# Two mixers of a four-layer fp32 network: weight chunks in another order, transposes that take turns by a table, and a key selection cut in three

## The chip, the cores and the metric

The kernel runs on one core of a Trainium2 chip. The metric is the device time of one launch in microseconds (us). The program computes, for one sequence of 256 tokens of width 1024, two layers of a first block and two layers of a second, and reads 458 MB of weights while it does so.

## The reference, cut to what matters

Every layer is a gated feed-forward, a mixer and a second feed-forward. The first block's mixer projects the normalized input to fifteen groups of columns and runs three attentions on them; the second block's mixer runs a state-space branch and one latent attention.

```
def hybrid_mixer(h, ...):                       # first block
    proj = h @ w_in
    (qa, ka, va, qi, ki, wi, qb, kb, vb, qc, kc, vc, ga, gb, gc) = jnp.split(proj, ...)
    qa, ka = rope(rmsnorm(qa)), rope(rmsnorm(ka)); qi, ki = rope(qi), rope(ki)
    o_a = dsa_attention(qa, ka, va, qi, ki, wi)  # index scores, the 64 best keys of each query, then attention
    o_b = moba_attention(rope(rmsnorm(qb)), rope(rmsnorm(kb)), vb)
    o_c = diff_attention(rope(rmsnorm(qc)), rope(rmsnorm(kc)), vc, lam, ...)
    merged = sigmoid(ga) * (o_a @ wa) + sigmoid(gb) * (o_b @ wb) + sigmoid(gc) * (o_c @ wc)
    return merged @ w_out

for l in range(2):                               # second block
    h = h + 0.5 * swiglu(rms_norm(h), ...)
    z, xbc, dt_raw, cq, ckv, kr, gates = split_cols(rms_norm(h) @ w_in, ...)
    y_ssd = ssd_branch(z, xbc, dt_raw, ...)      # causal convolution, chunked scan, norm, projection
    y_mla = mla_branch(cq, ckv, kr, ...)         # cq -> 8 heads of q, ckv -> k and v, rope, attention
    h = h + (g[:D] * y_ssd + g[D:] * y_mla) @ w_o
    h = h + 0.5 * swiglu(rms_norm(h), ...)
```

All of it is fp32. The kernel splits every weight and every activation into a high and a low part, and a product is three matmuls.

## The kernel before

The program is twelve phases: feed-forward, m1, feed-forward, feed-forward, m1, feed-forward for the first block and the same with m2 for the second. m1 is the first block's mixer (phases 1 and 4), m2 the second's (phases 7 and 10). Weights arrive as chunks of at most 1 MB (128 partitions, 2048 columns) in the order that chunk_list (L46) gives. The sync engine (SP) sends each chunk to one of five RAW slots; the scalar engine (ACT) rounds each half of it to WHI (`hi`, L1438, four slots); the vector engine (DVE) subtracts and writes the low part over RAW as WLO (`lo`, L2345); then TensorE (PE) multiplies. A chunk's slot is given back when PE has spent it.

Each engine runs a list of calls that is written out by hand (Tensor.m1 at L652, Scalar.m1, Vector.m1, Pool.m1, and the same for m2). An engine does its list strictly in order and meets the others by semaphores alone: `up` counts, `at` is the value to wait for. So a call that waits holds up all that is behind it on its engine.

m1 has 13 chunks called at (projections), then 12 called ag (gates), then ab and ao (output). A projection chunk j goes through these hands:

- PE: `at_`, four pieces of 12 matmuls (L390 to L392) into a PSUM bank;
- ACT: `tev`, copy to a staging slot of STA (three slots), and `psq`, squares to JUNK;
- DVE: `pss` (L2560, L2562), the sums of squares; for some chunks `kn` (L2571), which runs three Newton steps (L2350 to L2358) and scales the staging slot;
- GpSimd (POOL): `pg` (L3460, gain, and L3445 to L3449, rope, through RTA), and for the query chunks `prs` (L3477 to L3495), Newton steps on 128x8 numbers in 15 small instructions;
- PE: `ptr` (L518), four transposes of the staged slot, after which `sc` (scores, L557), `pt` and `pv` work on the attention's units 0 to 11: A (units 0, 1 and their like), B, then C from unit 6 on.

Between the index scores (`ix`, L535) and attention A stands the selection: `top`, eight rounds of MAX8 and MATCH_REPLACE8 on DVE (L2617, L2619) for each of two query blocks, 247.09 to 261.67 us.

m2 has four chunks bt (latent projections), 12 bx (convolution, `cv` L2922 on DVE), three bq and two bk (queries, keys and values from the latent), eight bz, and then bg, bs, bm, bo. Its q and k halves are staged in STB (four slots), transposed by `qtr`, `ktr` and `kptr` (helper L946), and the POOL engine does `qg` (L3573 and L3550 to L3554, gain and rope of a 128x512 tile), `rq` (L3582, L3584, the Newton steps, L3587) and `kp` (L3595). One PSUM bank serves all the transposes in turn, in the order of the table M2_TR.

Matmul groups are named by these lines: L379 to L381 are the gate, convolution and z chunks and the feed-forwards, L390 to L392 the projections.

Of the kernel before, what the change touches and what calls it, by code (L numbers as in the profile page):

```python
# [14 lines left out]
P = 128  # L15
# [29 lines left out]

def chunk_list(phases):  # L46

    out = []
    for kind, f in phases:
# [7 lines left out]
        elif kind == "m1":  # L57
            out += [("at", f, j) for j in range(13)]
            out += [("ag", f, j) for j in range(12)]
            out += [("ab", f, j) for j in range(3)] + [("ao", f, 0), ("ab", f, 3)]  # L60
            out += [("ao", f, j) for j in range(1, 4)]
        else:
            out += [("bt", f, j) for j in range(4)]
            out += [("bx", f, j) for j in range(8, 12)]
            out += [("bq", f, j) for j in range(3)]
            out += [("bk", f, j) for j in range(2)]
            for g in range(4):
                out += [("bx", f, 2 * g), ("bx", f, 2 * g + 1), ("bz", f, 2 * g), ("bz", f, 2 * g + 1)]
# [67 lines left out]
class Counts:  # L136
# [6 lines left out]
    def before(self, member, distance):  # L143
# [4 lines left out]
M1_ALL = (0, 1, 2, 3, 4, 5, 7, 8, 9, 10)  # L148
M1_BANK = Counts([0, 1] + list(range(3, 13)))
M1_STAGE = Counts(M1_ALL)  # L150
M1_SQUARE = Counts([2, 3, 4, 5, 7, 8, 9, 10, "sn0", "sn1"])
# [14 lines left out]
M1_TR = Counts(list(M1_ALL) + ["sn0", "sn1"])  # L166

M2_UNITS = [(0, (0, 2, 4, 6)), (0, (1, 3, 5, 7)), (1, (0, 2)), (1, (1, 3)), (1, (4, 6)), (1, (5, 7))]
M2_BANK = Counts([("bt", j) for j in range(4)] + [("bx", j) for j in range(8, 12)] + [("bq", j, t) for j in range(3) for t in range(2)]
                 + [("bk", j, t, h) for j in range(2) for t in range(2) for h in range(2)]  # L170
                 + [(kind, j) for g in range(4) for kind in ("bx", "bz") for j in (2 * g, 2 * g + 1)])
M2_TR = Counts([("lat", 0), ("lat", 1), ("lat", 2), ("cb", 0), ("cb", 1), ("q", 0, 0), ("cb", 2), ("q", 0, 1), ("cb", 3),
                ("q", 1, 0), ("q", 1, 1), ("dt",), ("btt",), ("q", 2, 0), ("q", 2, 1), ("k", 0, 0), ("k", 0, 1), ("kp", 0),
                ("k", 1, 0), ("k", 1, 1), ("kp", 1)]
               + [(kind, g) + c for g in range(4) for kind, c in (("xdt", (0,)), ("xdt", (1,)), ("s", ()), ("y", ()))])
# [4 lines left out]
M2_CONV = Counts(list(range(8, 12)) + list(range(8)))  # L180


def build(nc, phases, x_in, pos_in, w_in, cf_in, cm1_in, cm2_in, out, ctx):
# [61 lines left out]
    RTA = sb("RTA", [P, 2, 256], F32, at_kb(91.5))  # L245
# [109 lines left out]
    def m1_bank(j):  # L355
        return PS[6 if j == 2 else 4 + M1_BANK.index[j] % 2]

# [10 lines left out]
    class Tensor:  # L368
# [129 lines left out]
        def at_(self, n, j, t, p):  # L498
            e = self.e
            if t == p == 0 and j in M1_BANK.index and M1_BANK.index[j] > 1:  # L500
                e.wait_ge(*at("tev", n, M1_BANK.before(j, 2)))
            w = M1W[j]
            ins = self.columns(m1_bank(j)[:, t * 256:t * 256 + w], n, ck(n, "at", j), w, t, p, j == 0)
            ins.then_inc(*up("at", n, j, t, p))

        def ptr(self, n, j):
# [7 lines left out]
            if M1_TR.before(j, 1) is not None:  # L514
                e.wait_ge(*at("qt", n, M1_TR.before(j, 1)))
# [5 lines left out]
        def ix(self, n, t, u):  # L521
# [3 lines left out]
            if r == 0:  # L525
                e.wait_ge(*at("qt", n, 1))
                e.wait_ge(*at("qt", n, 2))
# [10 lines left out]
        def sc(self, n, i, x):  # L538
# [38 lines left out]
        def pv(self, n, i):  # L577
# [3302 lines left out]
```

## Time and profile before

| | us |
|---|---|
| median of three runs | 2791.62 (2791.45 to 2792.38) |
| the profiled execution | 2792.47 |
| its span | 2790.7 |
| mean granted clock of TensorE | 0.991 |
| PE busy | 2732.8 (98%) |
| DVE busy | 1788.0 (64%) |
| ACT busy | 1435.3 (51%) |
| POOL busy | 291.6 (10%) |

The span is the time from the first to the last instruction; some 1.8 us of the execution's own time lie outside of it. PE is the engine that works all the time, and the question of this kernel is where it does not: span less busy is 58 us. In the tables of stretches a row gives the length of the stretch and then, for each engine, busy time and number of instructions; the number behind the five engines is the granted clock of PE, 1.00 being 2.4 GHz and 0.5 being 1.2 GHz. POOL is nearly idle, and yet its small steps stand in chains on which PE waits.

### The profile page before, as it was taken

To read this page: it belongs to the slowest core of one execution; us is meant where nothing else is said; L and a number is where in the kernel's file an instruction comes from. 1 tells how busy PE (TensorE), PEld (TensorE's weight loads), DVE (VectorE), ACT (ScalarE), POOL (GpSimd) and SP (SyncE) were. 2 spreads that over 40 slices of the span, in tenths; PEclk is the share of its full clock that TensorE was granted. 3 is DMA by queue.
4 is the path that set the end of the run, shared out by engine and by line. 5 is a ranking of instruction groups with operands and counts; after the bars stand their busy time and mean duration, and the time that the engine had idled before them with its cause. 6 is when DMAs were issued, how large, how long until landed. Compare 5 with 4: busy or idle time off the path is not lost.

```text
span 2790.7 us, 48889 instructions
## 1 busy us (share of the span) xinstructions
PE 2732.8 (98%) x20056; PEld 2573.8 (92%) x20056; DVE 1788.0 (64%) x3060; ACT 1435.3 (51%) x2445; POOL 291.6 (10%) x446
## 2 busy tenths in 40 slices
PE   8999999999999999999999899999999999999999
PEld 8998999999998999999998899999999988999998
DVE  5558857456568856556558687565565596875654
ACT  5445645444445645445446575454454565854543
POOL 0005211000005210000002212100000022111000
PEclk9999999999999999999999999999999999999999
DMA  5453254554543344545444234554444442345453
GB/s 206 184 200 127 107 181 161 192 196 174 190 176 122 122 177 176 193 168 196 182 158 167 89 137 152 181 184 181 181 182 181 177 162 91 128 160 181 167 185 147
DMA packets 64733, 462.02 MB, mean 166 GB/s; under 512 B 7296, under 2 KB 7808, under 8 KB 9344
## 3 DMA queue, kind: packets, MB, share of 16 engines
q1 hardware_dynamic: 64512, 458.90, 44.9%
q8 instruction: 160, 2.62, 0.4%
q14 instruction: 61, 0.50, 0.1%
HBM read 457.83 MB, written 1.05 MB: 164 GB/s over the span
## 4 chain that ended last, share of the span: by engine, by line
PE 85%; POOL 5%; DVE 4%; issue 3%; ACT 1%; DMA 1%; SPq 0%; DVEq 0%; POOLq 0%; ACTq 0%
PE bank L457 17%; PE bank L379 17%; PE bank L381 17%; PE bank L380 17%; PE bank L390 3%; PE bank L392 3%; PE bank L391 3%; PE bank L645 3%; DVE WLO L2345 1%; DVE CV L2922 1%; PE bank L423 1%; DMA RAW<-weights_dram 1%; POOL STA L3460 1%; POOL SM L3485 1%; POOL SM L3483 0%
## 5 line engine op out<-in xcount | busy, mean ns | idle before, releaser
L2345 DVE TENSOR_TENSOR WLO<-RAW,WHI 128x1024 fp32r<-128x1024 f32 (+1 forms) x872 | 1056.9, 1251 | 282.4 <-ACT WHI L1438 281.0
L1438 ACT CAST WHI<-RAW 128x1024 fp32r<-128x1024 f32 (+1 forms) x872 | 885.5, 1047 | 374.9 <-DMA RAW<-weights_dram 238.4
L379 PE MATMUL bank<-XH,WHI 128*128 128x256 f32 x3712 | 1064.1, 287 | 4.0 <-DVE WLO L2345 4.0
L380 PE MATMUL bank<-XL,WHI 128*128 128x256 f32 x3712 | 1052.2, 283 | 0.0
L381 PE MATMUL bank<-XH,WLO 128*128 128x256 f32 x3712 | 1052.0, 283 | 0.0
L379 PEld LDWEIGHTS bank<-XH,WHI 128*128 128x128 f32 x3712 | 713.7, 192 | 13.1 <-issue 5.8
L380 PEld LDWEIGHTS bank<-XL,WHI 128*128 128x128 f32 x3712 | 713.9, 192 | 6.6 <-issue 1.4
L381 PEld LDWEIGHTS bank<-XH,WLO 128*128 128x128 f32 x3712 | 713.5, 192 | 0.0
L1502 ACT ACTIVATE SG<-bank 128x256 f32<-128x256 f32 x152 | 58.4, 384 | 481.9 <-PE bank L381 481.9
L2458 DVE TENSOR_TENSOR HF<-SG,bank 128x256 f32<-128x256 f32 x152 | 64.0, 421 | 339.1 <-ACT SG L1502 339.1
L390 PE MATMUL bank<-WHI,XH 128*128 128x256 f32 (+2 forms) x928 | 268.8, 290 | 5.0 <-DVE XL L2399 4.9
L392 PE MATMUL bank<-WHI,XL 128*128 128x256 f32 (+2 forms) x928 | 263.6, 284 | 0.0
L391 PE MATMUL bank<-WLO,XH 128*128 128x256 f32 (+2 forms) x928 | 263.5, 284 | 0.0
L457 PE MATMUL bank<-WHI,HH 128*128 128x512 f32 x704 | 219.4, 393 | 0.0
L457 PE MATMUL bank<-WLO,HH 128*128 128x512 f32 x704 | 217.8, 390 | 0.0
L457 PE MATMUL bank<-WHI,HL 128*128 128x512 f32 x704 | 217.4, 390 | 0.0
L390 PEld LDWEIGHTS bank<-WHI,XH 128*128 128x128 f32 x928 | 179.2, 193 | 7.3 <-issue 6.5
L391 PEld LDWEIGHTS bank<-WLO,XH 128*128 128x128 f32 x928 | 179.5, 193 | 0.4
L392 PEld LDWEIGHTS bank<-WHI,XL 128*128 128x128 f32 x928 | 179.4, 193 | 0.0
L457 PEld LDWEIGHTS bank<-WLO,HH 128*128 128x128 f32 x704 | 132.2, 188 | 29.0
L457 PEld LDWEIGHTS bank<-WHI,HL 128*128 128x128 f32 x704 | 132.2, 188 | 28.5
L457 PEld LDWEIGHTS bank<-WHI,HH 128*128 128x128 f32 x704 | 123.0, 189 | 17.0
(346 smaller groups left out, 3190.7 us busy)
## 6 DMA issues: line engine op xcount, KB each, us to landing
RAW<-weights_dram SPq DMA_DIRECT2D x431, 1024.0 KB, 4.8
RAW<-weights_dram SPq DMA_DIRECT2D x2, 800.0 KB, 4.2
X<-x_dram SPq DMA_DIRECT2D x2, 512.0 KB, 6.0
RAW<-weights_dram SPq DMA_DIRECT2D x2, 512.0 KB, 7.5
out_dram<-X SPq DMA_DIRECT2D x2, 512.0 KB, 2.7
RAW<-weights_dram SPq DMA_DIRECT2D x2, 384.0 KB, 3.2
CM<-mixer_dram SPq DMA_DIRECT2D x2, 320.5 KB, 9.8
CM<-mixer_dram SPq DMA_DIRECT2D x2, 176.0 KB, 5.3
```

What stands on the lines that cost most here:

```text
L379: self.e.matmul(bank, h, xh[:, x0 + k, :], start=k == k0, stop=False)
L380: self.e.matmul(bank, h, xl[:, x0 + k, :], start=False, stop=False)
L381: ins = self.e.matmul(bank, l, xh[:, x0 + k, :], start=False, stop=k == k1)
L390: self.e.matmul(bank, xh[:, x0 + k, xs], h, start=k == k0, stop=False)
L391: self.e.matmul(bank, xh[:, x0 + k, xs], l, start=False, stop=False)
L392: ins = self.e.matmul(bank, xl[:, x0 + k, xs], h, start=False, stop=k == k1)
L457: ins = e.matmul(PS[2 * t + nh][:, :], a[:, i % HR, t * P:t * P + P], w[:, c % s, col + nh * 512:col + nh * 512 + 512], start=i == 0 and w ...
L645: ins = e.matmul(PS[2 * t + h][:, :], a[:, k, xs], w[:, c % s, i * 1024 + h * 512:i * 1024 + h * 512 + 512], start=k == 0 and w is WHI and ...
L1438: e.copy(WHI[:, c % NHI, a:b], RAW[:, c % NLO, a:b]).then_inc(*up("hi", c, p))
L1502: e.activation(SG[:, i % 2, :], PS[5 - i % 2][:, 0:256], ACT.Silu).then_inc(*up("sg", n, i))
L2345: e.tensor_tensor(WLO[:, c % NLO, a:b], RAW[:, c % NLO, a:b], WHI[:, c % NHI, a:b].bitcast(F32), ALU.subtract).then_inc(*up("lo", c, p))
L2458: e.tensor_tensor(HF[:, r, :], SG[:, r, :], PS[5 - i % 2][:, 256:512], ALU.mult).then_inc(*up("hf", n, i))
```

## The change

The order of chunks in both mixers becomes a table, and banks, staging slots and waits are derived from the tables. In m1 the gate chunk ag0 now comes behind at11, ag1 to ag3 behind at5, ag4 and ag5 behind at12, and ag6 to ag11 at the end; the projections stand in the order 1, 0, 2, 3, 6, 9, 11, 4, 10, 5, 12, 7, 8. In m2, bx and bz chunks come between the latent chunks; bk1, which makes the second half of the keys' and values' input, is late. Attention C of m1 moves behind ag7. Transposes follow their own tables. RTA has three buffers in place of two. `top` takes the first and last round, and is called three times for each query block. The lists of the five engines follow from that. Cut to its core:

```
+M1_ORDER = [("at", 1), ("at", 0), ("at", 2), ("at", 3), ("at", 6), ("at", 9), ("at", 11), ("ag", 0), ("at", 4), ("at", 10), ("at", 5), ...]
+M1_TRANSPOSED = [0, 1, 2, 3, 9, 4, 10, 5, 7, 8]
+M2_ORDER = [("bt", 0), ..., ("bt", 3), ("bx", 9), ("bq", 0), ("bq", 1), ("bq", 2), ("bk", 0), ("bx", 8), ("bz", 0), ("bx", 0), ("bx", 1), ("bk", 1), ...]
+M2_TRANSPOSED = [("lat", 0), ("lat", 1), ("lat", 2), ("q", 0, 0), ("q", 0, 1), ("q", 1, 0), ("q", 1, 1), ("q", 2, 0), ("k", 0, 0), ("k", 0, 1), ("q", 2, 1), ("kp", 0), ...]
...
-            out += [("at", f, j) for j in range(13)]
-            out += [("ag", f, j) for j in range(12)]
+            out += [(k, f, j) for k, j in M1_ORDER]
...
-    RTA = sb("RTA", [P, 2, 256], F32, at_kb(91.5))
+    RTA = sb("RTA", [P, 3, 256], F32, at_kb(91.5))
...
+        def m1_tr_free(self, n, m):
+            if M1_TR.before(m, 1) is not None:
+                self.e.wait_ge(*m1_tr_read(n, M1_TR.before(m, 1)))
...
-        def top(self, n, t, rounds, end):
+        def top(self, n, t, a, z):
...
-            for _ in range(rounds):
+            for _ in range(a, z):
...
# Vector.m1
-            self.top(n, 0, 8, True)
+            self.top(n, 0, 0, 3)
+            self.top(n, 0, 3, 6)
+            self.top(n, 0, 6, 8)
             self.causal(n, 1)
-            self.top(n, 1, 8, True)
-            self.pss(n, 4)
-            self.pss(n, 5)
-            self.nb(n, 0)
-            self.pss(n, 7)
-            self.kn(n, 5)
+            self.top(n, 1, 0, 3)
+            self.top(n, 1, 3, 6)
+            self.top(n, 1, 6, 8)
+            self.pss(n, 9)
...
# Pool.m1
             self.prs(n, 3)
+            self.pg(n, 9)
+            self.prs(n, 9)
             self.pg(n, 4)
+            self.pg(n, 10)
+            self.prs(n, 4)
             self.pg(n, 5)
             self.pg(n, 7)
-            self.prs(n, 4)
             self.prs(n, 7)
             self.pg(n, 8)
-            self.pg(n, 9)
-            self.prs(n, 9)
-            self.pg(n, 10)
# Pool.m2
             self.qg(n, 1)
+            self.kp(n, 0)
             self.rq(n, 0)
+            self.kp(n, 1)
             self.rq(n, 1)
-            self.kp(n, 0)
-            self.kp(n, 1)
...
# Tensor.m1, behind the index scores
             self.ptr(n, 3)
+            self.at_(n, 9, 1, 0)
+            self.at_(n, 9, 1, 1)
+            self.at_(n, 11, 0, 0)
...
+            self.sc(n, 0, 0)
+            self.sc(n, 0, 1)
+            self.ag(n, 0, 0, 0)
...
+            self.ptr(n, 9)
+            self.at_(n, 4, 0, 0)
...
+            self.at_(n, 10, 1, 1)
+            self.ptr(n, 4)
```

Three places of the lists, first as before and then as changed. On DVE behind the selection of the first m1 (SBI is its result; JUNK holds the squares):

```order
L2622 TENSOR_SCALAR SBI<-ISC 128x256
L2560 TENSOR_REDUCE SM<-JUNK 128x8
L2562 TENSOR_SCALAR SM<-SM 128x8
L2560 TENSOR_REDUCE SM<-JUNK 128x8
L2562 TENSOR_SCALAR SM<-SM 128x8
L2636 TENSOR_REDUCE SM<-bank 128x2 x2
L2648 SCALAR_TENSOR_TENSOR SM<-SM 128x4
```

```order
L2657 MATCH_REPLACE ISC<-SM,ISC 128x256
L2660 TENSOR_SCALAR SBI<-ISC 128x256
L2598 TENSOR_REDUCE SM<-JUNK 128x8
L2600 TENSOR_SCALAR SM<-SM 128x8
L2383 TENSOR_TENSOR WLO<-RAW,WHI 128x1024 x6
L2598 TENSOR_REDUCE SM<-JUNK 128x8
L2600 TENSOR_SCALAR SM<-SM 128x8
L2383 TENSOR_TENSOR WLO<-RAW,WHI 128x1024 x2
L2674 TENSOR_REDUCE SM<-bank 128x2 x2
```

Six `lo` now stand directly behind one sum of squares (that of at9), and two more behind the next; before, the first `lo` came only behind three sums and the Newton steps of kn5. On POOL, from the last instruction of prs3 on (STA is the staging tile, RTA the rope's scratch, SM small numbers):

```order
L3495 TENSOR_SCALAR SM<-SM 128x8
L3460 TENSOR_TENSOR STA<-STA,CM 128x512
L3445 TENSOR_TENSOR RTA<-STA,CC_61 128x128
L3446 TENSOR_TENSOR RTA<-STA,SS_62 128x8x8
L3447 TENSOR_TENSOR RTA<-STA,SS_62 128x8x8
L3449 TENSOR_TENSOR STA<-RTA 128x8x16
L3460 TENSOR_TENSOR STA<-STA,CM 128x512
```

```order
L3549 TENSOR_SCALAR SM<-SM 128x8
L3514 TENSOR_TENSOR STA<-STA,CM 128x512
L3503 TENSOR_TENSOR RTA<-STA,CC_61 128x128
L3504 TENSOR_TENSOR RTA<-STA,SS_62 128x8x8
L3505 TENSOR_TENSOR RTA<-STA,SS_62 128x8x8
L3507 TENSOR_TENSOR STA<-RTA 128x8x16
L3531 TENSOR_SCALAR SM<-SM 128x8
L3532 TENSOR_SCALAR SM<-SM 128x8
L3535 TENSOR_TENSOR SM<-SM 128x8
```

Where pg5 followed pg4 directly, the 15 instructions of prs9 now stand between pg9 and pg4. On POOL in m2, around the first scaling of the keys' rope part, kp (STB is the staging tile):

```order
L3485 TENSOR_SCALAR SM<-SM 128x8
L3487 TENSOR_TENSOR SM<-SM 128x8
L3587 TENSOR_SCALAR SM<-SM 128x8
L3595 TENSOR_TENSOR STB<-SM_67,SM 128x512 x2
L3603 TENSOR_TENSOR JUNK<-XDT,SM_67 128x512
```

```order
L3608 TENSOR_TENSOR STB<-RT_122 128x512
L3653 TENSOR_TENSOR STB<-SM_67,SM 128x512
L3639 TENSOR_TENSOR SM<-SM 128x8
L3641 TENSOR_SCALAR SM<-SM 128x8
L3531 TENSOR_SCALAR SM<-SM 128x8
L3532 TENSOR_SCALAR SM<-SM 128x8
```

The first kp moved ahead of both rq and stands directly behind the second rope; the second kp stands between rq0 and rq1.

## Rows read from the trace of the kernel before

**Rows 1.** The page's busy times: engine, us, share of the span, instructions.
```profile
PE 2732.8 (98%) x20056; PEld 2573.8 (92%) x20056; DVE 1788.0 (64%) x3060; ACT 1435.3 (51%) x2445; POOL 291.6 (10%) x446
```
**Rows 2.** Stretches: both m1, a feed-forward, both m2; PE, PEld, DVE, ACT, POOL, clock, DMA.
```profile
203.00:450.00 247.00, 236.84 (x1813) 223.75 (x1811) 180.75 (x407) 136.93 (x259) 69.87 (x125) 0.99 0.41 145
450.00:637.00 187.00, 187.00 (x1334) 176.65 (x1333) 104.03 (x148) 87.16 (x130) 0.00 (x0) 1.00 0.50 183
826.00:1072.00 246.00, 236.71 (x1807) 223.63 (x1807) 180.62 (x404) 136.38 (x256) 69.85 (x125) 0.98 0.40 144
1448.00:1836.00 388.00, 375.12 (x2876) 352.71 (x2875) 290.13 (x507) 229.98 (x439) 73.46 (x95) 0.98 0.41 146
2212.00:2598.00 386.00, 371.97 (x2877) 350.05 (x2876) 290.39 (x508) 230.02 (x438) 73.41 (x95) 0.99 0.41 146
```
**Rows 3.** Waits of 203 to 450 us: who for whom, total, number, longest.
```profile
PE bank L518 <- DVE STA L2571: 5.6, 2, 5.2
```
**Rows 4.** DVE in time order, first m1: start, duration.
```profile
247.09 0.28 DVE L2617 MAX8 SM<-ISC 128x8 f32<-128x128 f32 x1
261.67 0.68 DVE L2560 TENSOR_REDUCE SM<-JUNK 128x8 f32<-128x512 f32 x1
269.88 2.36 DVE L2345 TENSOR_TENSOR WLO<-RAW,WHI 128x1024 fp32r<-128x1024 f32 x2
```
**Rows 5.** POOL in time order, first m1.
```profile
244.11 0.95 POOL L3433 MEMSET QT<- 128x1024 f32 x1 [4.64 <-PE bank L535]
245.15 0.44 POOL L3477 TENSOR_SCALAR SM<-SM 128x8 int32<-128x8 int32 x1
250.45 1.30 POOL L3460 TENSOR_TENSOR STA<-STA,CM 128x512 f32<-128x512 f32 x1
253.36 1.35 POOL L3460 TENSOR_TENSOR STA<-STA,CM 128x512 f32<-128x512 f32 x1
270.09 1.06 POOL L3483 TENSOR_TENSOR SM<-SM 128x8 f32<-128x8 f32 x1
```
**Rows 6.** PE in time order: two matmuls 48 apart in m1; transposes in m2.
```profile
256.66 0.28 PE L390 MATMUL bank<-WHI,XH 128*128 128x256 f32 x1
262.42 0.28 PE L390 MATMUL bank<-WHI,XH 128*128 128x256 f32 x1
1480.88 0.60 PE L913 MATMUL bank<-CF,CQ 128*128 128x128 f32 x4
1518.52 0.60 PE L946 MATMUL bank<-CF,STB 128*128 128x128 f32 x4
1521.73 0.60 PE L972 MATMUL bank<-BC 128*128 128x128 f32 x4
```
**Rows 7.** Stretches at a low granted clock, columns as in Rows 2.
```profile
268.00:276.00 8.00, 6.78 (x33) 5.09 (x34) 5.05 (x13) 2.12 (x4) 6.38 (x20) 0.57 0.01 2
1538.00:1542.00 4.00, 3.08 (x10) 1.73 (x8) 3.76 (x11) 3.37 (x5) 3.23 (x10) 0.57 0.01 2
1551.00:1559.00 8.00, 5.11 (x26) 5.11 (x27) 1.94 (x2) 1.70 (x3) 3.75 (x3) 0.57 0.01 2
2312.00:2320.00 8.00, 4.04 (x21) 4.04 (x21) 2.69 (x3) 1.16 (x2) 4.66 (x5) 0.57 0.00 0
```
**Rows 8.** PE's longest wait in m2: 1448 to 1836 us, then 2212 to 2598 us.
```profile
PE bank L946 <- POOL STB L3595: 4.9, 1, 4.9
...
PE bank L946 <- POOL STB L3595: 5.5, 1, 5.5
```
**Rows 9.** POOL in time order, first m2.
```profile
1523.14 1.30 POOL L3573 TENSOR_TENSOR STB<-STB,CM 128x512 f32<-128x512 f32 x1 [30.29 <-ACT STB L1951]
1530.49 1.29 POOL L3573 TENSOR_TENSOR STB<-STB,CM 128x512 f32<-128x512 f32 x1
1536.19 0.27 POOL L3582 TENSOR_TENSOR SM<-SM 128x8 f32<-128x8 f32 x1
1551.97 2.86 POOL L3595 TENSOR_TENSOR STB<-SM,SM 128x512 f32<-128x512 f32 x2
```

More of the change, by code:

```diff
@@ L145, in before @@
         return self.members[i] if i >= 0 else None
[L148 to L151, printed above, removed]
+M1_BANK = Counts([m for m in M1_ORDER if m != ("at", 2)])
+M1_STAGE = Counts([j for k, j in M1_ORDER if k == "at" and j not in (6, 11, 12)])
+M1_SQUARE = Counts([j for j in M1_STAGE.members if j > 1] + ["sn0", "sn1"])
 M1_IX = Counts([(0, 0), (1, 0), (1, 1), (0, 1), (1, 2), (1, 3)])
@@ L513, in ptr @@
                 e.wait_ge(*at("rope", n, j))
-            if M1_TR.before(j, 1) is not None:
-                e.wait_ge(*at("qt", n, M1_TR.before(j, 1)))
+            self.m1_tr_free(n, j)
             for i in range(2):
@@ L1097, in bg @@
             if a == u == 0:
-                e.wait_ge(*(at("z2", n, 6 + j) if j < 2 else at("gtt", n, j - 2)))
+                if j > 1:
+                    e.wait_ge(*at("gtt", n, j - 2))
+                elif j == 0:
+                    for m in M2_BANK.members[-3:]:
+                        e.wait_ge(*m2_read(n, m))
             if u == 0:
@@ L1190, in m2 @@
+            self.bx(n, 0, 0, 0)
+            self.kptr(n, 1)
+            self.bx(n, 0, 0, 1)
+            self.bx(n, 0, 1, 0)
+            self.btt(n)
+            self.msc(n, 0)
+            self.msc(n, 1)
+            self.bx(n, 0, 1, 1)
+            self.msc(n, 2)
+            self.mpt(n, 0)
+            self.bx(n, 1, 0, 0)
+            self.bx(n, 1, 0, 1)
+            self.msc(n, 3)
+            self.bx(n, 1, 1, 0)
+            self.msc(n, 4)
+            self.bx(n, 1, 1, 1)
             self.bk(n, 1, 0, 0)
-            self.qtr(n, 2, 1)
@@ new lines, in m1 @@
+            self.hi(c + 15, 1)
+            self.qt(n, 5)
+            self.hi(c + 16, 0)
+            self.ex(n, 1)
+            self.gtt(n, 2)
+            self.hi(c + 16, 1)
+            self.pe(n, 0)
+            self.oh(n, 0)
+            self.ex(n, 2)
+            self.pe(n, 1)
+            self.hi(c + 17, 0)
+            self.oh(n, 1)
+            self.ex(n, 3)
+            self.ex(n, 4)
+            self.pe(n, 2)
+            self.gtt(n, 3)
+            self.hi(c + 17, 1)
+            self.oh(n, 2)
@@ L3442, in turn @@
             cc, ss = cc1.to_broadcast([P, 2, nh, 16]), ss1.to_broadcast([P, 2, nh, 16])
-            if M1_STAGE.before(j, 2) is not None:
-                e.wait_ge(*at("rope", n, M1_STAGE.before(j, 2)))
+            if r == M1_STAGE.index[j]:
+                e.wait_ge(*at("lam", n))
+                if n == 1:
+                    e.wait_ge(*at("tab", 1))
             e.tensor_tensor(a, view[..., 0:16], cc, ALU.mult)
```

1318 lines of the change are left out of this document (657 added, 661 removed), and 3 rows, old and new, of the table M2_TRANSPOSED.

## The prediction

> **What bounds the kernel now.** I read the page's busy times first: PE is busy 2732.8 of a span of 2790.7 us, the next engine 64% and POOL 10% [rows 1]. The number of matmuls doesn't change, so what can be won is PE's idle time, 58 us, and whatever the clock costs. Then the stretches: a feed-forward has no idle time at all (187.00 of 187.00), the two m1 have 247.00 - 236.84 = 10.2 and 9.3 us, the two m2 12.9 and 14.0 us, together 46.4 us [rows 2]. All the change touches lies in these four stretches. The waits then say what ends the idle time: in m1 one wait of 5.2 us for the scaled staging tile of kn5 (L2571), beside nine of 0.2 to 1.0 us [rows 3]; in each m2 one of 4.9 or 5.5 us for POOL's kp [rows 8], beside a dozen of 0.2 to 1.5. Last I looked for stretches at a lower clock: 268 to 276, 1538 to 1542, 1551 to 1559 and 2312 to 2320 us show a mean granted clock of 0.57, most of each being at 1.2 GHz [rows 7]. Three of the four begin or lie right behind PE's long waits. What such a stretch costs is its excess over full pace. I count 2.9 us there, 1.4 us at 1538, 2.2 at 1551, 1.8 at 2312, each from the matmul starts in the stretch, 0.24 us apart against 0.12.
>
> **Durations.** Two matmuls 48 apart start 5.76 us apart, so a chunk of 48 costs PE 5.7 us and a quarter of it 1.42 [rows 6]. A transpose and half a q chunk (12 matmuls of 512 columns) take 3.21 us [rows 6], 0.36 and 2.85. One `lo` takes 1.18 us [rows 4]. The selection takes 261.67 - 247.09 = 14.6 us of DVE [rows 4]. On POOL the Newton steps of prs3 took 250.45 - 245.15 = 5.3 us, a gain and rope 253.36 - 250.45 = 2.9 us [rows 5]; in m2 the rope qg0 took 1530.49 - 1523.14 = 7.35 and qg1 1536.19 - 1530.49 = 5.7 us, and rq0 with rq1 1551.97 - 1536.19 = 15.8 us [rows 9].
>
> **The selection in three pieces.** The three calls stand directly behind one another, and DVE gets the same instructions in the same order. I cost it at nothing. What would have been done between the pieces (sums of squares, `lo`) still comes behind 14.6 us of selection.
>
> **m1.** The 5.25 us wait on kn5 goes, since at5's transpose now comes after ag1. What is late next is the transpose of at4. Count from T0, the end of the index scores, 244.1 [rows 5]. The selection ends at 261.7, T0+17.6, and the sum of squares of at9 at T0+18.4. POOL does prs9 next, and only then pg4. Its 15 small instructions run beside six `lo` that stand back to back on DVE. The row that bears on this is at 270.09: a small POOL instruction took 1.06 us, and it began just behind a `lo` that began at 269.88 [rows 4, 5]; the one behind it, beside the second `lo`, took as long, while those before and after took 0.20 to 0.28. So one small instruction goes by for each `lo`. By that, six instructions take 7.0 us, three in the reductions 0.9, two in the next two `lo` 2.3, and the last four 1.1: 11.3 us, to T0+29.7, and pg4 to T0+32.6. PE comes to that transpose after: transpose 3 (0.4), half of at9 (2.85), at11 (5.7), two scores (1.3), ag0 (5.7), transpose 9 (0.4), at4 (5.7), at10 (5.7), which is T0+27.7. It waits 4.9 us. Bounds: with prs9 at 5.3 us as prs3 was, pg4 ends at T0+26.6 and there is no wait; if all 15 take 1.1 us (16.5), pg4 ends at T0+37.8 and PE waits 10. I take 4.9, which the nearest row (270.09) gives.
>
> The Trainium skill ("GPSIMD Engine Reference", section "1. Specifications") says that POOL's SBUF interfaces are shared with VectorE, with contention beside vector instructions that have two SBUF inputs; `lo` is of that kind. The trace agrees, with 1.06 us in place of 0.20 for one instruction; by that rule 4.9 us is the wait, and without it the wait is zero.
>
> Behind the wait of 4.9 us the half-clock stretch of 268 to 276 stays in kind, behind a wait as long as before. The small waits: transposes 1, 8, 10 and the index scores lose some 1.6 us in sum (each was late behind its POOL rope); the transpose of at0 comes 0.7 us before its rope (it now also waits for lambda), and the score of unit 3, the first `pt` and transpose 8 gain some 1.5 us from the denser order. Sum: -5.25 + 4.9 - 1.6 + 0.7 + 1.5 = +0.2 us for each m1, with bounds of -8.2 (no wait, and 2.9 of the clock back) and +5.5. `lo` is otherwise covered: with the gate chunks in between DVE has at most half a microsecond more backlog at its worst than before, when it was 6.0 us.
>
> **m2.** The latent transpose 1 is at 1480.88 [rows 6]. From there: 0.36, half of bx9 2.85, 0.36, six q halves 17.1, four transposes 1.44: end of bq at 1503.0; four quarters of bk0 5.6: the transpose of q(2,0) at 1508.6. qg0 starts as soon as q(2,0) is copied, 1501.5 to 1502.5, and ends 7.35 later, about 1509.5; wait 1.4 us (0 to 2). qg1 ends 5.7 later, 1515.7, and kp0, 1.4 us of the 2.86 that both take [rows 9], at 1517.1; PE gets to its transpose, after five quarters of chunks and three transposes, at 1518.3, so the wait of 4.9 (5.5 in the second m2) [rows 8] goes. kp1 stands behind rq0, half of 15.8 us: 1517.1 + 7.9 + 1.4 = 1526.4, with PE there at 1525.2, four quarters and three transposes on. A wait of 1.2 (none if rq0 takes 5.3 like prs3; 10 if its 17 instructions take 1.1 each). Other waits: first k transpose 0.5, q(2,1) 0.8, btt 0.2, scores of unit 2 0.7, the tail 1.7; I take these from the nearest small waits of the stretch, 0.2 to 1.5. Sum 6.5 us against 12.9 and 14.0: a gain of 6.4 and 7.5. Bounds 3 and 16 us of waits. The half-clock stretches at 1538, 1551 and 2312, which stood behind these waits, go: 1.4 + 2.2 + 1.8 = 5.4 us; one of them might stay behind the wait of q(2,0), I keep 0.2 for it and count 5.2. The chunk in the first part of m2 at half clock (1473 to 1481) is behind narrow matmuls that the change leaves in place.
>
> DMA: the same chunks, the same bytes, one order for another; in the mixers the queue moves 144 to 146 GB/s against 183 in the feed-forward, which hides it without an idle PE [rows 2]. I cost it at nothing; if that cover is gone a late chunk costs PE 1 to 2 us once. The added waits are on events long past.
>
> **Sum.** Of the profiled execution's own time, 2792.5: -13.9 (m2 waits), -5.2 (clock), +0.4 (two m1) = 2773.8. This execution was 0.9 us above the median of 2791.6, so on the median 2773.
>
> **The rivals.**
> A. POOL keeps its pace beside `lo`: prs9 5.3 us, no wait at at4's transpose. For it: prs3 went at 0.20 to 0.48 an instruction while DVE ran the selection [rows 5]. Against it: the row at 270.09. Then each m1 gains 5.25 + 2.9 = 8.2 less 0.6 of small ones: 2773 - 2 x 7.8 - 2 = 2756.
> B. Slower. POOL's strict order: prs9 ahead of pg4 in m1, rq0 ahead of kp1 in m2, with every one of their instructions at 1.1 us beside `lo`. In m1 a wait of 10 us, 5 above what it was, with a half-clock stretch of 3 to 4 more; in m2, rq0 takes 18 us in place of 7.9, PE waits 10 us for kp1, where it was 5 for kp before, and 1 to 3 for the clock. Added up: 2 x (10 - 5.25 + 3.5 + 1) + 2 x (10 - 5.2 - 1 + 1) = 18 to 2809. It decides from the point at which such a step takes more than about 10 us beside DVE in m1 (the slack is 27.7 - 18.4 - 2.9 = 6.4 us) and 7 in m2. Against it: rq0 and rq1 took 15.8 us for 34 instructions [rows 9], 0.46 each, though DVE was busy beside them too.
> C. No change: m1 gets 5 us slower each by the wait and its clock, m2 gives back half of its gain since units and scan are now packed closer. 2773 + 10 + 8 = 2791.
> D. The pieces of the selection do not do what they say. That is my forecast already; were they to let work in between, at4's sums would be 7 us earlier and nothing on PE's path would change, as prs9 is ahead.
>
> **Chances.** Forecast 0.48 (2765 to 2782); A 0.25 (2752 to 2762); C 0.14; B 0.13. What a measurement of this kernel can tell from no change is 0.2%, 5.6 us. From the cases: faster 0.78 (the forecast, A, a little of C), same 0.12, slower 0.10. Eight in ten: A's lower part to C's, 2752 to 2789.
>
> **What would show it.** In the changed trace: PE's idle time in each m2 near 6.5 us, with no wait for kp0 above 1 us and none of 4 us for kp1; in m1 no wait for kn5, but one of 3 to 6 us for the rope of at4 (its transpose's releaser is POOL, L3507), with six or more of the small POOL instructions at 1.0 to 1.2 us behind T0+18; no stretch at half clock in the q/k part of m2. I'm wrong if at4's transpose doesn't wait, if m2's idle stays above 10 us, or if PE's idle time appears in the gate chunks, where it is zero now.

## The result, and the profile after

Measured against each other, the changed kernel has a median of 2763.92 us (2762.88 to 2766.84, four runs) and the kernel before 2791.53 us. The ratio is 0.9904, with a 95% interval of 0.9887 to 0.9921: 26.8 us less, 22 to 32. The forecast was 2773 with a range of 2752 to 2789; the gain is half as large again as the 18.6 us forecast. The profiled execution took 2763.72 us, its span is 2761.9.

Each feed-forward behind the first mixer takes 189.3 us in both traces, and the first one differs by 0.5 us. All the rest, 28.3 us, is in the mixers. A phase is cut here from its own first normalization to that of the next phase. These are the four mixers, first of the kernel before (phases 1, 4, 7 and 10; columns as in [rows 2]):

```profile
201.00:445.05 244.05, 233.89 (x1798) 221.28 (x1797) 177.79 (x398) 133.16 (x250) 69.87 (x125) 0.99 0.40 142
823.64:1067.46 243.82, 234.53 (x1798) 221.89 (x1797) 178.10 (x398) 133.38 (x250) 69.85 (x125) 0.98 0.40 142
1446.08:1831.16 385.08, 372.20 (x2862) 350.27 (x2861) 287.21 (x498) 226.24 (x429) 73.46 (x95) 0.98 0.41 144
2209.78:2592.78 383.00, 368.97 (x2862) 347.57 (x2861) 287.18 (x499) 226.21 (x430) 73.41 (x95) 0.99 0.41 145
```

and of the changed one:

```profile
200.60:441.74 241.14, 232.22 (x1798) 220.90 (x1797) 179.54 (x398) 132.95 (x250) 74.16 (x125) 0.99 0.41 144
820.31:1061.53 241.22, 232.71 (x1798) 221.77 (x1797) 180.23 (x397) 133.61 (x250) 74.55 (x125) 0.99 0.41 144
1440.12:1811.26 371.14, 364.55 (x2862) 345.39 (x2861) 286.74 (x499) 226.40 (x430) 75.22 (x95) 1.00 0.41 149
2189.88:2564.03 374.15, 368.30 (x2862) 349.44 (x2861) 286.78 (x498) 226.48 (x430) 74.45 (x95) 0.98 0.42 148
```

Three differences can be read from them. Length: -2.9, -2.6, -13.9 and -8.9 us. PE's idle time (length less busy time): 10.2 to 8.9, 9.3 to 8.5, 12.9 to 6.6 and 14.0 to 5.9, together 16.5 us less. Busy time, with the same matmuls: 11.8 us less, most of it in the first m2.

PE's waits in the changed kernel, in the first m1 (the four longest lines) and then in the first m2 (all). A line gives who waits for whom: total, number, longest. They answer to [rows 3] and [rows 8]; L565 and L965 are what L518 and L946 were, L3507 is the last step of the m1 rope, L3608 of the m2 rope, and L3083 scales a k tile on DVE:

```profile
PE bank L565 <- POOL STA L3507: 4.4, 3, 3.9
PE bank L565 <- DVE STA L2609: 1.2, 1, 1.2
PE bank L423 <- DVE MTA L2752: 1.0, 1, 1.0
PE bank L605 <- DVE SBI L2660: 0.7, 1, 0.7
...
PE bank L965 <- DVE STB L3083: 4.7, 1, 4.7
PE bank L965 <- POOL STB L3608: 0.9, 1, 0.9
PE bank L1120 <- POOL SACC L3674: 0.6, 1, 0.6
PE bank L932 <- DVE CQ L2932: 0.3, 1, 0.3
```

The waits for kn5 and for kp are gone. In m1 a wait of 3.9 us for POOL's rope stands in the place of kn5's 5.25; in m2 four waits are left of a dozen, and one of them, 4.7 us for the scaled k tile, stood in the forecast as 0.5 us.

The stretches at a low clock, in the changed kernel, to be held against [rows 7] (same columns); behind them three of the kernel before that [rows 7] does not have:

```profile
276.00:284.00 8.00, 5.26 (x32) 5.26 (x33) 7.01 (x16) 3.30 (x10) 7.36 (x14) 0.79 0.30 123
896.00:904.00 8.00, 5.85 (x30) 5.85 (x31) 7.04 (x15) 3.30 (x10) 7.36 (x14) 0.57 0.28 115
1504.00:1512.00 8.00, 3.97 (x23) 3.97 (x24) 7.76 (x12) 1.75 (x3) 6.27 (x7) 0.79 0.08 32
2216.00:2228.00 12.00, 12.00 (x78) 12.00 (x78) 8.22 (x25) 7.98 (x14) 3.56 (x9) 0.72 0.37 137
2256.00:2268.00 12.00, 7.88 (x48) 7.89 (x49) 9.36 (x15) 3.94 (x7) 9.37 (x19) 0.72 0.06 25
```

```profile
888.00:900.00 12.00, 8.20 (x35) 6.00 (x36) 8.70 (x25) 5.51 (x16) 9.87 (x29) 0.57 0.17 69
1472.00:1484.00 12.00, 12.00 (x79) 12.00 (x79) 10.10 (x43) 9.35 (x15) 0.00 (x0) 0.72 0.38 141
2236.00:2244.00 8.00, 8.00 (x58) 8.00 (x58) 6.10 (x22) 5.93 (x12) 0.00 (x0) 0.79 0.51 197
```

I count as the cost of the clock half of what PE was busy while it ran at 1.2 in place of 2.4 GHz. In the changed kernel that is 1.7 + 2.6 + 1.4 + 3.4 + 2.6 = 11.6 us (rounded terms); before, the same count gives 3.0 and 4.0 us in the two m1, 7.2 and 3.6 us in the two m2, 17.8 us in all. So 16.5 us of the 28.3 us in the mixers are idle time, 6.2 us the clock, and 5.6 us are busy time at full clock, to which I come back below.

### The profile page after: what moved, and what is told of

It is laid out like the page before. It is cut to its first block and busy times, and to the rows that moved or that the text cites. A ratio compares the mean times of both kernels' runs of the same rounds, so it can differ in the third digit from the quotient of the medians.

```text
span 2761.9 us, 49011 instructions
## 1 busy us (share of the span) xinstructions
PE 2721.2 (99%) x20056; PEld 2570.8 (93%) x20056; DVE 1791.2 (65%) x3060; ACT 1435.9 (52%) x2445; POOL 303.4 (11%) x446
## 5 line engine op out<-in xcount | busy, mean ns | idle before, releaser
L423 PEld LDWEIGHTS bank<-XH,WHI 128*128 128x128 f32 x3712 | 713.8, 192 | 11.2 <-issue 5.0
```

The source lines that it names most:

```text
L423: self.e.matmul(bank, h, xh[:, x0 + k, :], start=k == k0, stop=False)
```

## The experiments

All kernels ran against the kernel before. The table has the medians, the ratio to the kernel before with its interval, and the lengths of the four mixer phases in each one's trace, cut as above. Differences of a phase by under 2 us say little: the low-clock stretches alone make them. Each trace is one execution; that of kernel 1 is the fastest of its nine, 2779.8 us and so 7 us below its median, and its phases add up to more gain than the kernel has.

| kernel | us | ratio | m1, m1 | m2, m2 |
|---|---|---|---|---|
| before | 2791.5 | | 244.1, 243.8 | 385.1, 383.0 |
| changed | 2763.9 | 0.9904 (0.9887 to 0.9921) | 241.1, 241.2 | 371.1, 374.2 |
| 1 m1 alone | 2786.8 | 0.9983 (0.9972 to 0.9993) | 242.0, 240.3 | 379.8, 383.0 |
| 2 m2 alone | 2770.1 | 0.9927 (0.9914 to 0.9941) | 244.1, 243.0 | 372.8, 371.6 |
| 3 before, kp first | 2779.5 | 0.9960 (0.9947 to 0.9972) | 244.6, 243.1 | 379.5, 376.1 |
| 4 changed, kp last | 2776.6 | 0.9950 (0.9936 to 0.9964) | 240.8, 240.3 | 379.8, 379.2 |
| 5 prs9 behind at7's rope | 2766.6 | 0.9914 (0.9900 to 0.9928) | 243.8, 243.1 | 372.9, 372.0 |
| 6 prs9 behind at5's rope | 2752.6 | 0.9865 (0.9849 to 0.9882) | 235.8, 235.2 | 373.5, 372.2 |
| 7 at9's sum between pieces | 2756.8 | 0.9875 (0.9862 to 0.9889) | 236.9, 236.8 | 375.1, 372.2 |
| 8 low parts with one input | 2758.3 | one run | 237.2, 236.8 | 374.1, 373.5 |
| 9 kp0 ahead of qg1 | 2764.6 | 0.9907 (0.9892 to 0.9922) | 241.0, 241.2 | 373.3, 372.5 |
| 10 edits of 6 and 9 | 2756.2 | 0.9875 (0.9860 to 0.9890) | 235.6, 235.2 | 376.9, 372.7 |
| 11 and low parts later | 2753.7 | 0.9866 (0.9853 to 0.9880) | 235.9, 235.3 | 373.0, 373.0 |
| 12 and bx8 earlier | 2754.1 | 0.9862 (0.9846 to 0.9879) | 235.5, 235.2 | 373.9, 374.1 |

**1 and 2: which mixer pays.** Each takes all of the change that belongs to one kind of mixer, tables, waits and the lists of five engines.

> The kernel before with the new order in the two m1 alone; both m2 as before. Theory: the mixers do not act on each other, so this gives what the traces of before and after differ by in the m1 phases, 2.9 and 2.6 us, together 5.5 us less than before (2786), with the wait of 3.9 us for the rope of at4 still there and none for kn5. Rival: the change in m1 as a whole is worth nothing, as I forecast (+0.4), and the 5.5 us come from the clock falling differently: then 2790 to 2793. Second rival: what m1 does ahead of m2 decides when the clock falls later, and the m2 phases here change too, by over 2 us.

> The kernel before with the new order in the two m2 alone. Theory: 14.0 + 8.9 = 22.9 us less than before (2769), with the wait of 4.7 us for the scaled k tile in each m2, and m1 phases of 244 us as before. Rival: part of m2's gain was the clock's, which fell once less in the first m2; then the low stretches fall differently here and the gain is 17 to 20 us.

m1 alone gives 4.7 us (1.9 to 7.8), m2 alone 20 us (16 to 24); the sum, 25 us, is the change within its interval. m1 was worth something, against my +0.4. The second rival is half right: the first m2 of kernel 1, with an unchanged list, took 379.8 us in place of 385.1 in the one execution traced. Its wait for kp was 1.0 us where the kernel before has 4.9, and the second m2's was 5.5 as before. POOL began kp0 102.6 us into that phase, against 105.9 in the kernel before, half of it because the Newton steps of rq1 took 7.3 us in place of 9.2; PE asked for it at 103.5 and 102.9. So this wait, and not the clock alone, comes out differently in the same program text; the wide spread of kernel 1's times (2780 to 2792) would fit that, but only one of them has a trace.

**3 and 4: the order on POOL in m2.** Kernel 3 edits only this, in the kernel before; kernel 4 takes it back out of the changed one.

```
# Pool.m2                 before -> kernel 3     (kernel 4: the same, turned round)
+            self.kp(n, 0)
             self.rq(n, 0)
+            self.kp(n, 1)
             self.rq(n, 1)
-            self.kp(n, 0)
-            self.kp(n, 1)
```

> The kernel before, with one edit: on POOL in m2 the scalings kp0 and kp1 stand ahead of rq0 and of rq1, as in the changed kernel. Theory A (the POOL order alone takes the long wait away, the order of chunks gives the rest): the waits of 4.9 and 5.5 us go, with the low-clock stretch behind them (2.4 and 1.9 us), about 13 to 15 us less, 2777, but small waits of 0.2 to 1.5 us in m2 stay. Theory B (the wait only moves: kp0 must wait for the scaled keys or kp1 for rq0): 2 to 6 us less, 2786 to 2789, with a wait of 3 us or more for kp1. Theory C (nothing without the chunk order): the same as before within 2 us.

> The changed kernel, with POOL's order in m2 as before: rq0, rq1, then kp0 and kp1. Theory (the order on POOL is needed also with the new order of chunks): kp0 comes at 1521 to 1524 us where PE asks for it at 1516.4, so a wait of 4 to 7 us in each m2, beside the 4.7 us for the scaled keys, with 2 us of low clock: 2763.9 + 2 x 7 = 2778, 2772 to 2782. Rival (the new chunk order alone gives the slack, and the edit on POOL that was worth 11.5 us on the old order is worth nothing on the new one): 2763 to 2767.

Two moved lines give 11.2 us of the 26.8 (7.8 to 14.8). In kernel 3 kp0 starts at 1539.08 and no wait for kp is left in either m2, as theory A has it. The gain is a little below its 13 to 15: the first m2 still has two low-clock stretches (1536 to 1540 and 1543 to 1547, 3.4 us together) where the kernel before has two at 1538 and 1552 (3.8 us). On the new order of chunks the same lines are worth 12.7 us (2776.6 less 2763.9). Kernel 4's waits in the first m2:

```profile
PE bank L965 <- POOL STB L3653: 4.9, 1, 4.9
PE bank L965 <- DVE STB L3083: 4.7, 1, 4.7
PE bank L1120 <- POOL SACC L3674: 1.0, 1, 1.0
PE bank L965 <- POOL STB L3608: 0.9, 1, 0.9
```

The wait for kp is back at the 4.9 us it had before, though each chunk around it stands elsewhere. Of the 20 us that m2 alone gives, that leaves some 8 to 9 us for the order of chunks and transposes. No kernel has this order alone; kernel 4, which has it with the change in m1, is 14 us below the kernel before, and less the 4.7 us of m1 that is 9 us too.

**5, 6 and 7: the 15 small instructions of prs9.** In the changed kernel they stand ahead of at4's rope. Kernels 5 and 6 move them on POOL; kernel 7 leaves POOL alone and feeds them earlier.

```
# Pool.m1       changed          kernel 5          kernel 6
                pg 9             pg 9              pg 9
                prs 9            pg 4              pg 4
                pg 4             pg 10             pg 10
                pg 10            prs 4             prs 4
                prs 4            pg 5              pg 5
                pg 5             pg 7              prs 9
                pg 7             prs 9             pg 7
                prs 7            prs 7             pg 8
                pg 8             pg 8              prs 7
# Vector.m1, kernel 7
             self.top(n, 1, 0, 3)
+            self.pss(n, 9)
             self.top(n, 1, 3, 6)
             self.top(n, 1, 6, 8)
-            self.pss(n, 9)
```

> The changed kernel, with one edit: on POOL in m1 the 15 small instructions of prs9 stand behind the rope of at7 in place of ahead of the rope of at4. Theory (prs9, slowed by the low-part subtractions beside it, delays that rope): the 3.9 us waits at at4's transpose go, with the low-clock stretches behind them (1.3 and 2.5 us), and 0.5 us each comes back at the transpose of at10: 2763.9 - 2 x 3.4 - 3.8 = 2753. Rival (the wait moves on to the transpose of at10, whose scaling on the vector engine and rope on POOL then are last): a wait of 3 us or more there, and 2762 to 2764.

> The changed kernel, with POOL's m1 list edited: prs9 stands behind the rope of at5, where POOL had nothing to do for tens of us, and the rope of at8 ahead of prs7. The run with prs9 behind the rope of at7 took the 3.9 us wait at at4's transpose down to 1.2, and a new wait of 5.5 us for at8's scaled tile took its place, with 2.6 us of low clock behind it. Theory (it is only a question of which rope stands behind the 15 small instructions): the wait at at4 is 1.2 us, that at at8 under 0.5, no low-clock stretch in either m1, so 2763.9 - 2 x 4.0 - 3.7 = 2752, with 2750 to 2756. Rival (a wait at this density of work always finds another place, at10 or at5 or the scores that need the factor of at7): a new wait of 3 us or more in m1, and 2762 to 2767.

> The changed kernel, with one edit: the sum of squares of at9 (two instructions on the vector engine, 0.85 us) stands between the first and the second piece of the second query block's selection in place of behind the last. It is the first use of the cut in pieces. Theory (what hurts in m1 is that prs9's 15 instructions meet eight back-to-back low-part steps, while MAX8 and MATCH_REPLACE8 hold nothing up): prs9 starts some 7 us earlier, takes 5 to 6 us, and is done when the low-part steps begin; the wait at at4's transpose falls from 3.9 to 1 to 1.5 us, the low-clock stretch behind it goes: 2763.9 - 2 x 2.7 - 3.7 = 2755, 2753 to 2758. Rival (selection also holds POOL up, or the squares of at9 are late): a wait of 3 us or more stays and the time is 2762 to 2766.

Kernel 5 was a miss with a use: 2766.6 us, where 2753 was expected. The wait at at4 fell from 3.9 to 1.2 us, and one of 5.5 us came up at a place I hadn't thought of, for at8's tile, whose rope now stood behind both prs9 and prs7. The rows name DVE (L2609, the scaling of that tile), but DVE itself had waited 8.6 us for POOL's rope. Kernel 5's waits in the first m1, then kernel 6's:

```profile
PE bank L565 <- DVE STA L2609: 5.5, 1, 5.5
PE bank L565 <- POOL STA L3507: 1.7, 3, 1.2
PE bank L423 <- DVE MTA L2752: 1.0, 1, 1.0
```

```profile
PE bank L565 <- POOL STA L3507: 1.7, 3, 1.1
PE bank L423 <- DVE MTA L2752: 1.0, 1, 1.0
PE bank L605 <- DVE SBI L2660: 0.6, 1, 0.6
PE bank L693 <- DVE XL L2759: 0.6, 1, 0.6
PE bank L565 <- DVE STA L2609: 0.5, 1, 0.5
```

In kernel 6 nothing above 1.1 us is left, there is no low-clock stretch in either m1, and the m1 phases are 5.3 and 6.0 us shorter than in the changed kernel: 2752.6 where 2752 was expected. Its ratio to the kernel before, 0.9865, has an interval that ends below the changed kernel's 0.9887, so it beats both. Kernel 7 gets nearly there (2756.8; 2755 expected) by the cut in pieces alone: prs9 begins at 258.73, 5.8 us earlier, beside MAX8 and MATCH_REPLACE8, and its instructions take 0.20 to 0.24 us each, all 15 in 4.4 us.

**8: what on DVE holds POOL up.** The eight `lo` behind the selection of each m1 become a product by 1 of RAW, with one input. What they write is the whole weight; this kernel leaves out the low parts of those chunks, and serves for its times alone.

```
-            e.tensor_tensor(WLO[...], RAW[...], WHI[...], ALU.subtract)
+            e.tensor_scalar(WLO[...], RAW[...], 1.0, None, ALU.mult)
```

> The changed kernel, in which the eight low-part steps behind the selection in each m1 are a product by 1 of RAW alone (one input from SBUF) in place of RAW minus WHI (two inputs); what they write is the whole weight and not its low part. Theory (two SBUF inputs on the vector engine are what holds POOL's small instructions up, as for the reductions and MAX8, which have one and hold up nothing): the 15 instructions of prs9 take 5 us in place of 11.3, and the wait at at4's transpose is below 1 us. Rival (any long instruction of the vector engine on 1024 columns holds them up, or a one-input fp32 instruction does so too where it runs in a faster mode): 1.0 us or as long as the instruction beside it, and a wait of 3 to 4 us.

The rival holds for what blocks POOL, and the theory for the wait. DVE, then POOL, in kernel 8 (start, duration):

```profile
264.75 3.71 DVE L2389 TENSOR_SCALAR WLO<-RAW 128x1024 fp32r<-128x1024 f32 x6
```

```profile
266.76 0.54 POOL L3541 TENSOR_TENSOR SM<-SM 128x8 f32<-128x8 f32 x1
267.38 0.53 POOL L3543 TENSOR_TENSOR SM<-SM 128x8 f32<-128x8 f32 x1
267.99 0.55 POOL L3545 TENSOR_SCALAR SM<-SM 128x8 f32<-128x8 f32 x1
268.63 0.20 POOL L3547 TENSOR_TENSOR SM<-SM 128x8 f32<-128x8 f32 x1
```

The one-input form runs at 0.62 us each, about half of the 1.15 of `lo`. Beside six of them POOL got five instructions done, four of 0.53 to 0.56 us and one of 1.11, in place of 0.20 to 0.24. So this one-input fp32 instruction blocks POOL too, only for half as long, and two inputs are not what it takes. This fits the other half of the sentence of the Trainium skill ("GPSIMD Engine Reference", section "1. Specifications"), contention beside instructions in a 2-port performance mode; that the instruction ran in such a mode is not shown here, only its pace. prs9 took 6.7 us in place of 11.3, and no wait above 0.4 us for POOL's rope was left.

**9 to 12: the other direction.** The 4.7 us wait in m2 is for rk0, 13 small DVE instructions, and the scaling of the first k half behind them. Why is it late? In the changed kernel, DVE and then POOL in the first m2:

```profile
1501.31 1.26 DVE L2389 TENSOR_SCALAR SM<-SM 128x8 f32<-128x8 f32 x1
1502.61 0.17 DVE L2392 TENSOR_TENSOR SM<-SM 128x8 f32<-128x8 f32 x1
1502.81 1.14 DVE L2394 TENSOR_TENSOR SM<-SM 128x8 f32<-128x8 f32 x1
1507.29 1.29 DVE L3083 TENSOR_TENSOR STB<-STB,SM 128x512 f32<-128x512 f32 x2
```

```profile
1501.25 1.30 POOL L3629 TENSOR_TENSOR STB<-STB,CM 128x512 f32<-128x512 f32 x1
1502.62 1.30 POOL L3604 TENSOR_TENSOR RT<-STB,CC 128x512 f32<-128x512 f32 x1
```

The DVE instruction that starts at 1501.31 ends at 1502.57, with POOL's (1502.55). The next slips in between, and the one at 1502.81 ends at 1503.95, again with POOL's (1503.92). rk0 took 7.5 us from 1499.80 on; rk1, beside POOL's small instructions, 2.6. Kernel 9 swaps kp0 and qg1 on POOL. Kernel 10 has that and kernel 6's edit. Kernel 11 adds this on DVE, and kernel 12 moves bx8's step ahead of one `lo` and a z step:

```
# Vector.m2, kernel 11
             self.rk(n, 0)
-            self.lo(c + 10, 1)
-            self.lo(c + 11, 0)
-            self.lo(c + 11, 1)
             self.kss(n, 1, 0)
             self.kss(n, 1, 1)
+            self.lo(c + 10, 1)
             self.rk(n, 1)
+            self.lo(c + 11, 0)
+            self.lo(c + 11, 1)
# kernel 12
             self.cv(n, 8)
             self.lo(c + 12, 0)
+            self.xs_(n, 8)
             self.lo(c + 12, 1)
             self.z2(n, 0)
-            self.xs_(n, 8)
```

> The changed kernel, with one edit: on POOL in m2 kp0 stands ahead of the second rope qg1. kp0 waits for the scaled keys, so POOL stands still while the vector engine does the 13 small instructions of rk0, which took 7.5 us beside qg1 and 2.6 us where POOL had small work only. Theory (POOL's 128x512 instructions hold the vector engine's small ones up, one for one): rk0 takes 2.5 to 3 us, the wait of 4.7 us at the first k transpose is gone, and a new one of 2.5 to 3.5 us comes at the transpose of q(2,1), which now waits for qg1; net -1.2 to -2.2 us for each m2, perhaps 1.4 to 2.5 of clock each: 2756 to 2761. Rival (rk0 is slow for a reason of its own, waits between its steps or late sums of squares): rk0 again takes 7 us or more, kp0 and then qg1 come later still, and the time is 2770 or more.

> Both edits on POOL together, prs9 behind the rope of at5 with at8's rope ahead of prs7 in m1, and kp0 ahead of qg1 in m2. Theory (the mixers are independent): the sum of the two single gains, 2752 less 3 to 8, so 2744 to 2749, which would be faster than both kernels. Rival: rk0 is not helped, and the time is that of the m1 edit alone or above it, 2752 to 2760.

> The kernel with both edits on POOL (prs9 behind at5's rope, kp0 ahead of qg1), and one more on the vector engine in m2: the three low-part steps behind rk0, which took 6.5 us beside qg1 while qg1 took 8.1, now stand behind the sums of squares of the second half of the keys. Theory (POOL's and the vector engine's long instructions run one at a time, so that two of them beside each other each take twice as long): qg1 takes 5.3 us, the wait for it at the transpose of q(2,1) falls from 5.7 to 2.5 to 3.5 us, and its low-clock stretch may go; against the 2756.2 of both edits this gives 2756.2 - 2 x 2.5 - 2 = 2749, 2746 to 2753, with up to 1.5 us each given back where chunk bz0 waits for its low part. Rival (the wait is only passed on, to bz0's low part or to the second half's keys): 2754 to 2758.

> The kernel with both POOL edits and the three low-part steps of m2 moved behind the keys' sums of squares, with one more edit on the vector engine: the second half of chunk bx1's low part and the z step stand behind the convolution step of bx8 in place of ahead of it. The last run left a new wait of 1.4 us in each m2, for that convolution step at the transposes of the state inputs. Theory: those 1.4 us go and nothing else moves: 2753.7 - 2.8 = 2751, 2748 to 2753. Rival (the queue of the vector engine is full there, and the time is passed on to a low part or to the first scores): 2753 to 2756, within what a measurement can tell of the last one.

Kernel 9 shows the mechanism and no gain. rk0's Newton steps took 0.17 us each, and all of rk0 3.5 us in place of 7.5 (2.5 to 3 expected; one instruction still met the end of qg0). But the three `lo` behind it now met qg1. DVE and POOL of kernel 9:

```profile
1503.09 6.50 DVE L2383 TENSOR_TENSOR WLO<-RAW,WHI 128x1024 fp32r<-128x1024 f32 x3
```

```profile
1504.04 2.27 POOL L3629 TENSOR_TENSOR STB<-STB,CM 128x512 f32<-128x512 f32 x1
1506.38 2.12 POOL L3604 TENSOR_TENSOR RT<-STB,CC 128x512 f32<-128x512 f32 x1
1508.47 1.70 POOL L3605 TENSOR_TENSOR RT<-STB,SS 128x256 f32<-128x256 f32 x1
```

Three `lo` took 6.5 us (3.5 alone) and qg1 8.1 (5.4 in the changed kernel), and PE's wait for qg1's tile at q(2,1) became 5.7 us where I expected 2.5 to 3.5. The wait had only changed its name, and the 3 to 8 us that I expected from kernel 9 did not come (2764.6 against 2763.9). So kernel 10 missed as well: 2756.2 where 2744 to 2749 was expected, 3.5 us above kernel 6 (the intervals overlap), with a wait of 5.7 us in each m2. With the `lo` out of the way (kernel 11) the same POOL steps are:

```profile
1493.69 1.29 POOL L3629 TENSOR_TENSOR STB<-STB,CM 128x512 f32<-128x512 f32 x1
1495.06 1.29 POOL L3604 TENSOR_TENSOR RT<-STB,CC 128x512 f32<-128x512 f32 x1
1496.31 0.72 POOL L3605 TENSOR_TENSOR RT<-STB,SS 128x256 f32<-128x256 f32 x1
```

and the wait was 2.9 us, in the expected 2.5 to 3.5. Of the time, 2.5 us were won against kernel 10, where 7 were expected and the two intervals overlap; a new wait of 1.4 us in each m2 for bx8's step took some of it. Kernel 12 took that one away and met another, 1.0 us for the attention weights (ACT), and the time is that of kernel 11, as the rival had it. Neither is measurably faster than kernel 6. The m2 edits stop paying there.

## Why the prediction was right, and where it was not

**m1, the new wait: right, by its own steps.** The end of the selection was forecast at T0+17.6 and measured at 263.5 less 245.6, T0+17.9. The rows that count in the changed kernel, DVE, POOL and PE (start, duration):

```profile
264.30 6.90 DVE L2383 TENSOR_TENSOR WLO<-RAW,WHI 128x1024 fp32r<-128x1024 f32 x6
```

```profile
264.48 1.09 POOL L3531 TENSOR_SCALAR SM<-SM 128x8 int32<-128x8 int32 x1 [10.13 <-DVE SM L2600]
271.34 0.20 POOL L3535 TENSOR_TENSOR SM<-SM 128x8 f32<-128x8 f32 x1
271.91 1.31 POOL L3539 TENSOR_SCALAR SM<-SM 128x8 f32<-128x8 f32 x1
275.78 1.26 POOL L3514 TENSOR_TENSOR STA<-STA,CM 128x512 f32<-128x512 f32 x1
```

```profile
278.74 1.12 PE L565 MATMUL bank<-CF,STA 128*128 128x128 f32 x4 [3.94 <-POOL STA L3507]
```

prs9 took 275.78 - 264.48 = 11.3 us, the figure of the forecast: six instructions at 1.02 to 1.09 beside six `lo`, two beside the reduction at 0.20, two beside the next pair of `lo`, and the last five at 0.20 to 0.24. The wait was 3.9 us and not 4.9, because PE came 1.5 us later than T0+27.7 and the rope ended 0.5 us later than T0+32.6.

**m1, the sum: wrong by 3 us each.** The terms 4.9, +0.7 and +1.5 were mis-sized: the wait took 3.9, the transpose of at0 had none above 0.2, and the small waits of the first scores came to 0.7 + 0.3; at8's, 1.2, was the only one that my 1.5 had rightly foreseen. Idle time fell by 1.2 and 0.8 us, where the forecast had it rise by 0.2. The low-clock stretch, which I left at 2.9, was 1.7 in the first m1 and fell from 4.0 to 2.6 in the second, whose stretch (889 to 900) I had not listed. Busy time at full clock gave the other 0.4 us in each.

**m2, the wait for kp: right.** It goes with POOL's order, and experiments 3 and 4 give that order 11 to 13 us, waits and clock together. My reading, 4.9 and 5.5 us and the 2.2 and 1.8 us of the stretches behind them, is 14.4 us, at the upper end of the 7.8 to 14.8 us of kernel 3. q(2,0) waited 0.9 us (forecast 1.4, though its own times give 0.3 to 1.3) and kp1 not at all (1.2).

**m2, the remaining waits: right in sum and wrong in parts.** 6.5 us were forecast and 6.6 and 5.9 measured, and that is chance. "First k transpose 0.5" was 4.7. I had read POOL's slowing beside DVE in a row, and not asked for the reverse: DVE's rk0 beside POOL's qg1. Against it, five waits that I had counted did not come, or hardly (btt, unit 2, q(2,1), kp1 and most of the tail, 0.6 us of 1.7).

**The clock: near in size, 6.2 for 5.2 us, and not in its places.** I said that no half-clock stretch would be left in the q/k part of m2; both m2 have one there, behind the wait of 4.7 us (1508 to 1511, 1.4 us, and 2258 to 2265, 2.6 us). And I said that the stretch behind bt's narrow matmuls stays. It cost 3.4 and 1.7 us before, and nothing and 3.4 after, with the same matmuls ahead of it; in kernels 6 to 12 it was anything from nothing to 3.4. Single traces can't tell that term to better than 3 us, and two m2 made my sum look more certain than it was.

**Left out: busy time of PE at full clock.** 5.6 us of the gain are there, and the forecast had no term for it. 4.9 us of them are in the two m2, and they go with the order of chunks and transposes: less the cost of the clock, PE is busy 365.0 to 365.5 us in each m2 of the three kernels with the old order (before, 1 and 3), and 362.3 to 364.0 us in each m2 of the eleven with the new one, kernel 4 with POOL's old order among them. From start to start, the 48 transposes from STB take 5.4 us in an m2 before and 4.3 after, so 2.2 us are theirs. The ends of matmuls are modelled in the profile, and pauses too short to show as idle may be the rest; no run here tells. Of the 9.6 us between the forecast's 18.7 and the 28.3 us of the mixers in the traces, 5.6 are this term, 3.0 idle time (2.4 of it in m1) and 1.0 the clock.

**The rivals.** A (no wait in m1) was priced at 2756, and kernels 6 and 7, which bring it about by other means, came to 2752.6 and 2756.8; but they also have in them what the forecast left out, so the nearness is in part luck. B needed POOL's rq0 to take 18 us; it took 7.6 in the changed kernel and 8.4 in kernel 4. B's terms also add up to 28 us and not 18, so to 2819; A's give 7.6 us for each m1 where its sum takes 7.8, and no row shows the 2 us that it takes off besides. C wanted each m1 5 us slower and m2 to give back half: neither came. D was half right: the pieces do nothing as they stand, but I wrote that work between them would change nothing on PE's path. Kernel 7 shows the contrary, since the sum to put there is at9's and not at4's: prs9 begins 5.8 us earlier and is done before the first `lo`.

## What to carry to other kernels

Where PE is 98% busy, look for the few instructions of the idle engines that stand in its chains, and order those: here two moved lines on an engine that is 10% busy were worth at least as much (11 to 13 us over both m2) as the new order of all the mixer's chunks (8 to 9 us). Of each small serial chain (a Newton iteration) ask two things: what stands behind it in its engine's queue and could go ahead, and what the other of VectorE and GpSimd runs at that time, in both directions. Moving a step out of one overlap pays only if the place it goes to is free; otherwise the wait changes its name.

## What the runs showed of the hardware

- In the pairs below VectorE and GpSimd took turns by whole instructions, in both directions. A 128x8 instruction of either, 0.17 to 0.24 us alone, took 1.0 to 1.3 us beside the other engine's long one (`lo`, or POOL's 128x512) and ended within 0.1 us of its end. Long beside long, both slow down: `lo` from 1.17 to 2.17 us each, POOL's 128x512 from 1.29 to 2.27.
- Not all VectorE instructions do it. Beside MAX8 and MATCH_REPLACE8 (kernel 7) and beside a TENSOR_REDUCE at 271.13 in the changed kernel (POOL's row 271.34, above) POOL's took 0.20 to 0.24 (two of prs3 beside the selection in the changed kernel took 0.44 and 0.45); beside a one-input fp32 TENSOR_SCALAR of 1024 columns most took 0.55, nearly as long as that instruction itself (0.62).
- The stretches of PE at 1.2 GHz cost 1.4 to 4.0 us each. Of the 43 waits of 2.9 us and more inside a mixer in the fourteen traces, 42 had one at or right behind them (the other is one of kernel 12's two waits of 2.9 us), but waits of that length weren't needed: in the kernel before and in kernel 3 one began behind waits of 1.1 and 0.7 us close to each other (1536 to 1538); and one came and went behind the 96-column matmuls of m2 with no wait at all.
